# Two block-one weight remainders per layer computed by GpSimd instead of VectorE

## The reference

```python
    e = p_i @ w_ple_proj
    h = h + rms_norm(jax.nn.sigmoid(h @ w_ple_gate) * e, g_ple_post)
    return h
...
    u = rms_norm(h, g_mix_pre)              # next block-one layer
    ... = jnp.split(u @ w_in, offsets, axis=-1)
...
        x = x + 0.5 * swiglu_ffn(rms_norm_2(x, ffn1_norm[i]), ffn1_w_in[i], ffn1_w_out[i])   # block two
```

## Time and profile before

| | before |
|---|---|
| median of 3 runs | 2289.01 us |
| profiled execution | 2288.87 us, its span 2287.0 us |
| PE busy | 2264.5 us, 99% |
| DVE busy | 1573.0 us, 69% |
| ACT busy | 1318.2 us, 58% |
| POOL busy | 42.7 us, 2% |

### The profile page before, as it was taken

One profiled execution on the slowest core, in us unless ns is written; L12 is line 12 of the kernel. 1 busy time (PEld: TensorE's weight loads), 2 busy tenths in 40 slices (PEclk: granted clock), 3 DMA queues, 4 the chain that ended last, 5 costly groups with the idle time before them and its releaser, 6 DMA issues.

```text
span 2287.0 us, 31063 instructions
## 1 busy us (share of the span) xinstructions
PE 2264.5 (99%) x13008; PEld 1993.2 (87%) x13008; DVE 1573.0 (69%) x1799; ACT 1318.2 (58%) x1797; POOL 42.7 (2%) x76
## 2 busy tenths in 40 slices
PE   8999999999999999999999999999999999999998
PEld 8898898878988888788898889888888898989886
DVE  6866777478766775667577767674766678667755
ACT  6665655476655655565458755554654558555544
POOL 1000000010000000010000000000100000000000
PEclk9999999999999999999999999999999999999999
DMA  7725555557345655566555455555665655455553
GB/s 225 228 66 184 185 193 190 184 188 230 96 148 184 203 186 192 184 205 195 182 179 168 128 185 193 191 195 184 209 202 176 203 159 172 141 191 184 185 193 120
DMA packets 323514, 411.90 MB, mean 180 GB/s; under 512 B 11600, under 2 KB 245456, under 8 KB 323376
## 3 DMA queue, kind: packets, MB, share of 16 engines
q1 hardware_dynamic: 318160, 394.68, 53.0%
q0 software_dynamic: 4928, 14.26, 2.0%
q10 hardware_dynamic: 288, 0.99, 0.1%
HBM read 408.85 MB, written 1.05 MB: 179 GB/s over the span
## 4 chain that ended last, share of the span: by engine, by line
PE 93%; DVE 3%; ACT 2%; DMA 1%; issue 1%; SPq 0%; DVEq 0%; ACTq 0%
PE banks L608 27%; PE banks L616 14%; PE banks L687 10%; PE banks L686 10%; PE banks L685 10%; PE banks L592 4%; PE banks L593 4%; PE banks L594 4%; DVE lo L1760 1%; PE banks L736 1%; DMA raw<-in_w_in 1%; ACT hi L1179 1%; PE banks L862 1%; PE banks L871 1%; PE banks L1094 1%
## 5 line engine op out<-in xcount | busy, mean ns | idle before, releaser
L1760 DVE TENSOR_TENSOR lo<-raw,hi 128x2048 fp32r<-128x2048 f32 (+1 forms) x382 | 858.4, 2250 | 528.8 <-ACT hi L1179 524.7
L1179 ACT ACTIVATE hi<-raw 128x2048 fp32r<-128x2048 f32 (+1 forms) x382 | 716.0, 1878 | 255.8 <-DMA raw<-in_ffn_w_out 85.1
L608 PE MATMUL banks<-x_in,hi 128*128 128x512 f32 x2304 | 537.7, 390 | 0.0
L608 PEld LDWEIGHTS banks<-x_in,hi 128*128 128x128 f32 x2304 | 427.9, 188 | 85.8 <-issue 0.4
L616 PEld LDWEIGHTS banks<-x_in,lo 128*128 128x128 f32 x2304 | 286.6, 192 | 5.8 <-issue 0.2
L616 PE MATMUL banks<-x_in,lo 128*128 128x256 f32 x2304 | 289.3, 283 | 0.0
L592 PE MATMUL banks<-x_in,hi 128*128 128x256 f32 x736 | 210.7, 286 | 0.0
L594 PE MATMUL banks<-x_in,lo 128*128 128x256 f32 x736 | 208.5, 283 | 0.0
L593 PE MATMUL banks<-x_in,hi 128*128 128x256 f32 x736 | 208.4, 283 | 0.0
L685 PE MATMUL banks<-hi,x_hid 128*128 128x512 f32 x528 | 206.2, 390 | 0.0
L687 PE MATMUL banks<-hi,x_hid 128*128 128x512 f32 x528 | 205.7, 390 | 0.0
(11 more groups left out here) (341 smaller groups left out, 3080.7 us busy)
## 6 DMA issues: line engine op xcount, KB each, us to landing
raw<-in_w_in SPq DMA_DIRECT2D x108, 1024.0 KB, 5.2
raw<-in_ffn_w_in SPq DMA_DIRECT2D x88, 1024.0 KB, 5.1
raw<-in_w_ffn_in SPq DMA_DIRECT2D x44, 1024.0 KB, 5.1
raw<-in_ffn_w_out SPq DMA_DIRECT2D x40, 1024.0 KB, 5.1
raw<-in_w_ffn_out SPq DMA_DIRECT2D x20, 1024.0 KB, 5.2
raw<-in_w_o_gla SPq DMA_DIRECT2D x8, 1024.0 KB, 5.1
raw<-in_w_o_attn SPq DMA_DIRECT2D x8, 1024.0 KB, 5.1
raw<-in_w_out SPq DMA_DIRECT2D x8, 1024.0 KB, 5.1
```

Source lines behind the costliest of these rows:

```text
L608: mm = pe.matmul(bank[b + f], wh[:, k, f * P:(f + 1) * P], x[:, k, :, :].rearrange("p n s -> p (n s)"), start=(start and k == 0), stop=(k ...
L1179: act_fn(high, of, ACT.Copy).then_inc(hi_done.up(), 1)
L1760: tt(rest, of, parts(tile, hi)[0].bitcast(F32), ALU.subtract).then_inc(lo_done.up(), 1)
```

## The change

Four remainders, tiles 78 and 79 of both block-one layers, leave DVE's order. Its `pump` stops ahead of them. POOL computes them at the end of its part of the layer: for each it waits until the remainder before it is done and the tile's high part is there, and subtracts, raising the same `lo_done`. DVE waits at the start of the next layer until both are done.

```diff
                 row(1, dram["g_ple_post"][layer], 1)
+                for tile in line_of(1, layer)[-AHEAD:]:
+                    pool.wait_ge(*lo_done.at(tile.index))
+                    pool.wait_ge(*hi_done.at(tile.index + 1))
+                    rest, of = parts(tile, lo)
+                    nc.gpsimd.tensor_tensor(rest, of, parts(tile, hi)[0].bitcast(F32),
+                                            ALU.subtract).then_inc(lo_done.up(), 1)
...
                 while made[0] <= min(upto, len(layer_tiles[0]) - 1):
                     tile = layer_tiles[0][made[0]]
+                    if where.part == 1 and made[0] >= len(layer_tiles[0]) - AHEAD:
+                        made[0] = len(layer_tiles[0])
+                        break
...
                 made[0], layer_tiles[0] = AHEAD, line_of(1, layer)
+                dve.wait_ge(*lo_done.at(AHEAD))
...
                 made[0], layer_tiles[0] = AHEAD, line_of(2, layer)
+                dve.wait_ge(*lo_done.at(AHEAD))
```

## The result

The changed kernel takes 2301.06 us (median of 4 runs, 2300.65 to 2302.07) beside 2288.81 us before in the same session: 12.25 us slower, a ratio of 1.0053 with a 95% interval of 1.0041 to 1.0065. The profiled execution took 2301.09 us, its span 2299.3 us, 12.3 us over that of before.

A forecast was written before the change was run, and what follows sets the result against it. Both tails were taken as a DVE-ACT-PE latency chain without PE slack; holds of 4.2 and 4.3 us, together 8.4 by formula, plus 0.6 for hand-overs, gave +9.0 on 2288.87: 2298 us, range 2290.5 to 2302.5.

The forecast's parts named there:

- What is removed is worth at most 0.8 us: Four DVE remainders of about 2.3 us leave both tails; at most 0.8 us gained, 0.7 by ending a PE wait.
- D = 4.5 us: Time of one POOL subtraction of a tile's remainder, taken midway between 3.6 and 5.4 us.
- DVE is held, layer 0 at 2D - 4.8 = 4.2 us: End of layer 0: DVE's two-SBUF-input instructions start only when POOL ends, so `xn` reaches PE 4.2 us late.
- Layer 1, 4.3 us: End of layer 1: third `gated` held +2.3 us, tile 79's remainder at 976.9 instead of 972.62, +4.3 us in all.
- Hand-overs, 0.6 us: POOL's start after what it waits for: 0.15 us at each of four subtractions, bounds 0 to 3.2 in all.
- rival 3: Blocking plus something on top, a lower PE clock behind gaps (about 4.6 us) or D of 5.4: 2302 to 2307, chance 0.15.
- The ISA instruction and the DMAs moved past cost nothing: On POOL's queue and behind layer 1's subtractions: no cost, unless the ISA instruction delays the first subtraction.
- the forecast's own theory: POOL blocks DVE in both tails, D between 3.6 and 5: 2298 us, own range 2293.7 to 2301, chance 0.60.
- its formula: Loss of 2D - 4.8 per layer, 4D - 9.6 = 8.4 us together, plus 0.6 us of hand-overs.
- L2233 had no idle of 2 to 4 us ahead of it: Sign for blocking: DVE's L2233 would stand idle 2 to 4 us beforehand though its sigmoid was done.
- Rival 1: POOL does not hinder DVE, D = 4.5; layer 0 net -0.2, layer 1 +2.0 us: 2291 us, chance 0.18.
- rival 2: POOL as quick as DVE, D about 2.3, holding nobody; layer 0 keeps its 0.8 us gain: 2288 us, chance 0.07.

The follow-up runs named there:

- e1_memset: The changed kernel with GpSimd filling each of the four remainders with zeros twice in place of subtracting: 2291.19 us, 1.0009 of the kernel before.
- e7_copy: The changed kernel with GpSimd copying the raw tile over its remainder in place of subtracting, one SBUF input: 2288.14 us, 0.9996 of the kernel before.
- e3_warm: The changed kernel with PE transposing the identity where it stands idle in the two tails: 2298.03 us, 1.0040 of the kernel before.
- e2_contend: The kernel before, with GpSimd also subtracting two SBUF inputs into spare memory at the four places, not needed before the next layer: 2305.87 us, 1.0074.

## Why the prediction was right, and where it was off

It said 2298 us with a range of 2290.5 to 2302.5 and slower at 0.73; 2301.06 was measured.

- *What is removed is worth at most 0.8 us.* Right: without the hold, layer 0 gained 0.8 us (`e1_memset`).
- *D = 4.5 us.* The figure is right, 4.55 to 4.62; that its working led there was luck. It took the midpoint of "reads in turn" and "all three streams in turn", each stream at the memset's 1.83 us. But with one input and one output POOL took 1.90 us (`e7_copy`), hardly more than the 1.81 of a fill, so reading and writing don't take turns; and two inputs took over twice that. No run shows what makes it so.
- *DVE is held, layer 0 at 2D - 4.8 = 4.2 us.* Right. The third product started 2.2 us late (485.29 for 483.09), the t = 1 rows of `xn` were there at 498.69 + 0.69 = 499.38, 4.5 us after the 494.87 of the earlier trace rows.
- *Layer 1, 4.3 us.* The first hold came as reckoned: the third product ended at 966.87, 2.4 us late once layer 0's 5.6 are taken off. PE went on with tile 79 at 983.27, 10.6 us after the 972.67 of the earlier trace rows, so 5.0 in this layer: 0.7 over. That is three things. The delay did not pass whole: before, ACT was still loading its table when the third product was done (959.41 against 958.90), and this 0.5 us of slack, which the prediction counted against the gain, it did not take off the delay; the t = 1 rows of `xn` came only 1.9 us late. Tile 79's own part cost 2.2 us and not 2.0, of which 0.15 is the hand-over. The rest, 0.9 us, is the clock. Behind its first transposes this kernel has PE turn the identity 22 times; before, and then now:

```profile
964.12 2.56 PE L913 MATMUL banks<-cst 128*128 128x128 f32 x22
967.02 0.66 PE L736 MATMUL banks<-cst,xn 128*128 128x128 f32 x4 [0.34 <-DVE xn L1799]
```

```profile
972.01 3.63 PE L919 MATMUL banks<-cst 128*128 128x128 f32 x22
975.48 0.60 PE L742 MATMUL banks<-cst,xn 128*128 128x128 f32 x4
```

Now they run at the lower clock, and `xn`, there at 973.76 + 0.69 = 974.45, waits for PE until 975.48; ACT's high part of tile 79 comes behind these transposes. From the end of the third product to that high part took 11.2 us before, 11.7 in the changed kernel, and 10.7 in `e3_warm`, at full clock.

- *Hand-overs, 0.6 us.* POOL started 0.14 to 0.16 us behind each of the four high parts, as the 0.15 had it. A held instruction ends 0.54 to 0.55 us behind POOL, less than the 0.69 us that it takes by itself, so no more is lost there.
- *The clock.* This is the term that was mis-sized: nothing in the forecast, 4.6 us as part of rival 3 at 0.15. In layer 0, from `xn` to the roots' transposes took 508.04 - 499.38 = 8.7 us, 7.5 before: 1.1 more. It is where the prediction let PE's wait ahead of L680 overlap the same delay: its work from there took 3.15 us before, without the wait for `xn`, and 4.50 now (496.17 to 500.67), so that `xn` found PE still busy. In layer 1, from tile 79's start 10.7 against 9.2: 1.5 more. With the 0.9 above that is 3.5, beside the 3.0 to 3.5 us that `e3_warm` gave back. The prediction itself had PE standing 2 to 3 us at a time where it had never stood over 1.11, so that the gap could cost something behind it as well should have had a share in the sum. Without the clock the forecast is 2298, and `e3_warm`, where it is taken away, is at 2298.03.
- *The ISA instruction and the DMAs moved past cost nothing.* Right: the first subtraction started at 480.20, and outside the two tails 0.2 us were lost.

So 2301.06 lies in the range, but at the edge of what the forecast's own theory was given (2293.7 to 2301; the top has no working, and its formula gives 2299.9 for D = 5). What happened is that theory and a smaller form of rival 3's clock together. The signs named ahead say the same: POOL's rows and PE's waits were there, and so was rival 3's, matmuls spaced wider. One sign was wrong: L2233 had no idle of 2 to 4 us ahead of it with its sigmoid done, since the hold is inside the row. And the reading of layer 1's tail left out two of PE's waits for `xn`, of 0.73 and 0.34 us; the sum did not use them.

Rival 1 (no hindrance) is refuted by the stretched rows and by `e2_contend`, rival 2 by D. What stays open: when a wait of PE brings the clock down, and why one subtraction takes POOL 4.55 us and another 3.6.

## What to carry to other kernels

Before moving work to GpSimd, ask what VectorE does meanwhile: if both read SBUF and VectorE's instructions have two inputs there, the work isn't beside VectorE's but ahead of it, and twice as long. An idle engine and a busy one say nothing of that; the place in the chain does. And where a change makes PE wait longer than it did, look at the granted clock behind the gap too: here some 3 of the 12 us lay there, though not every such wait brought it down.

## What the hardware showed that was not expected

- A held DVE instruction shows as a long one (0.69 us as 4.72), not as an idle engine; the engines behind it show the wait.
- POOL subtracting a tensor from itself took 3.60 to 3.62 us where DVE did not delay it, from another of the same size 4.55. The first also lay elsewhere in SBUF; the runs don't separate the two.
- Cut in eight, POOL's subtraction took 0.72 to 1.23 us a piece, and 5.55 us for a whole tile with no two-input instruction of DVE beside it, where the uncut subtraction took 4.55:

```profile
978.33 5.55 POOL L539 TENSOR_TENSOR lo<-raw,hi 128x256 fp32r<-128x256 f32 x8 [7.97 <-ACT hi L1188]
```
